# Squared-ReLU layers with seven block products for eight, the weight sums on GpSimd

## The chip, the cores and the metric

The kernel runs on one core of a Trainium2 chip. The metric is the device time of one execution in microseconds (us), the median of several runs. Engines: TensorE (PE; PEld is its weight load), VectorE (DVE), ScalarE (ACT), GpSimd (POOL) and SyncE (SP), which issues the weight loads.

## The reference, cut to what matters

A chain of transformer blocks works on 256 tokens of width 1024. Two of its layers, one behind the latent and neighbourhood attention and one behind the dilated attention, are these:

```python
def sq_relu_mlp(xn, w1, w2):
    return jnp.square(jax.nn.relu(xn @ w1)) @ w2
...
x = x + sq_relu_mlp(rms_norm_2(x, norm_mlp[layer]), mlp_w1[layer], mlp_w2[layer])
```

w1 is 1024 x 4096, w2 is 4096 x 1024, all in float32. After the second layer comes a last norm.

## The kernel before, in words

Every product is kept near float32 accuracy by splitting both operands into a high part (fp32r) and the rest: `split_mm` (L1876 to L1881) issues high x high, high x low and low x high, each a matmul with a weight load of its own. ScalarE makes the high part of a weight tile with a copy (`high`, L627, the copy on L630), VectorE makes the low part by subtracting it from the raw tile (`low`, on L1056).

A squared layer (`mlp(l)`, on each engine) runs in 16 stages of 256 hidden channels. In a stage, `up` makes 256 hidden channels x 256 tokens: 2 halves x 8 blocks of the width x 3 = 48 matmuls of 256 columns, into bank 4 or 5. ScalarE applies the ReLU (L907); VectorE squares it, copies it to fp32r and subtracts (`split_hidden`, L1317, L1318, L1056). `down` multiplies the two 128-token tiles by the two 128-channel blocks and the two 512-column halves of the output, 8 block products x 3 = 24 matmuls of 512 columns. They add up in banks 0 to 3 over the 16 stages. `up` of one stage stands ahead of `down` of the stage before, so that the hidden values are made while TensorE is at work.

The raw weights of a stage are 2 MB in two loads; they lie in one of 4 slots of `weight_pool`. SyncE fetches them (`fetch_ring`) in the order written out; a slot is free once VectorE has made the low part of the down weights (`loD_ready`). High and low parts lie in `work`, two stages deep. In a step ScalarE makes the up weights two stages ahead, then, once `w_used` tells that `down` of the stage before is over, the down weights one stage ahead. VectorE follows it.

After the last stage `update(n, t)` (L1509) adds the banks to the residual, tile by tile, each with the scale of the tokens from the raw norm. The first half of it runs during the last `down` (`y_half`). Then TensorE turns the residual (`turn_raw`), ScalarE and VectorE write it as high and low (`raw_high`, `raw_low`), and the next part starts: dilated attention behind the first layer, the last norm and the output behind the second. On ScalarE and VectorE the first weights of the dilated attention, `od_high(0, 0, 0)` and `od_low(0, 0, 0)`, stand ahead of that update. GpSimd has no work in the two layers.

## Time and profile before

| | us |
|---|---|
| median of 3 runs | 1247.07 |
| lowest, highest | 1246.1, 1250.47 |
| profiled execution, its own time | 1248.23 |
| its span, first to last instruction | 1246.3 |
| TensorE busy in the span | 1184.4 (95%) |
| VectorE busy | 732.6 (59%) |
| ScalarE busy | 547.1 (44%) |
| GpSimd busy | 52.9 (4%) |

The median is the figure to compare. The span leaves out what lies around the first and the last instruction. Matmuls are pipelined, so the duration of one is longer than the time from its start to the next one's; a stage of TensorE is read from starts. An average over the span hides that the parts of the kernel have different limits.

### The profile page before, as it was taken

What the parts mean: (1) busy time and instruction counts of PE and PEld (TensorE: products, weight loads), DVE (VectorE), ACT (ScalarE), POOL (GpSimd) and SP (SyncE); (2) the same over time, 40 slices, a digit from 0 to 9 for tenths busy, and PEclk for the clock granted to TensorE, in tenths of its full rate; (3) what the DMA queues carried; (4) which work ended last, traced back from release to release, by engine and by line L of the source; (5) the groups of instructions that cost most, each with busy time, mean ns of one, the idle gap of its engine ahead of it and who ended that gap; (6) DMA issues with size and microseconds to landing.
All of it is one profiled execution on the core that took longest, in us unless ns stands there. A gap on an engine that the chain in (4) does not pass through costs nothing.

```text
span 1246.3 us, 18678 instructions
## 1 busy us (share of the span) xinstructions
PE 1184.4 (95%) x7356; PEld 1014.8 (81%) x7359; DVE 732.6 (59%) x971; ACT 547.1 (44%) x723; POOL 52.9 (4%) x60
## 2 busy tenths in 40 slices
PE   3899998999999989899999999999999999999997
PEld 1477785689999978647999998999999984999996
DVE  1569336474555576755465466777777765654653
ACT  3763243353434362644343345555555534433432
POOL 2000023000000070000000000000000000000000
PEclk9999999999999989999999999999999999999999
DMA  9673470899565550616645534455555254645410
GB/s 320 237 271 115 166 270 7 288 246 288 173 182 159 160 150 1 233 38 238 209 172 190 186 102 136 124 147 152 151 151 147 77 198 161 244 162 205 175 64 34
DMA packets 201039, 209.71 MB, mean 168 GB/s; under 512 B 5804, under 2 KB 166839, under 8 KB 200791
## 3 DMA queue, kind: packets, MB, share of 16 engines
q1 hardware_dynamic: 197520, 201.61, 51.2%
q0 software_dynamic: 1648, 5.03, 1.4%
q10 hardware_dynamic: 1814, 2.30, 0.6%
q8 instruction: 39, 0.64, 0.3%
q14 instruction: 18, 0.14, 0.0%
HBM read 207.86 MB, written 2.01 MB: 168 GB/s over the span
## 4 chain that ended last, share of the span: by engine, by line
PE 86%; DVE 7%; DMA 4%; ACT 2%; issue 2%; DVEq 0%; SPq 0%; ACTq 0%
PE bank L1879 21%; PE bank L1880 21%; PE bank L1881 21%; DMA weight_pool<-in_mod_w_dram 4%; PE bank L1726 3%; PE bank L1728 3%; PE bank L1727 3%; PE bank L2133 2%; PE bank L2274 2%; PE bank L2262 1%; PE bank L2252 1%; DVE work L1448 1%; PE bank L1683 1%; PE bank L2243 1%; PE bank L2233 1%
## 5 line engine op out<-in xcount | busy, mean ns | idle before, releaser
L1879 PE MATMUL bank<-hT_high,mlp_up_high 128*128 128x256 f32 x512 | 145.2, 284 | 1.1 <-DVE hT_low L1350 1.1
L1881 PE MATMUL bank<-hT_high,mlp_up_low 128*128 128x256 f32 x512 | 144.9, 283 | 0.0
L1880 PE MATMUL bank<-hT_low,mlp_up_high 128*128 128x256 f32 x512 | 144.9, 283 | 0.0
L1879 PE MATMUL bank<-od_w_high,hT_high 128*128 128x384 f32 x384 | 132.7, 346 | 1.6 <-DVE hT_low L1350 1.4
L1881 PE MATMUL bank<-od_w_high,hT_low 128*128 128x384 f32 x384 | 128.7, 335 | 0.0
L1880 PE MATMUL bank<-od_w_low,hT_high 128*128 128x384 f32 x384 | 128.5, 335 | 0.0
L1056 DVE TENSOR_TENSOR mlp_down_low<-weight_pool,mlp_down_high 128x2048 fp32r<-128x2048 f32 x32 | 73.3, 2289 | 59.2 <-ACT mlp_down_high L630 59.2
L1879 PE MATMUL bank<-hT_high,ffn_up_high 128*128 128x256 f32 x352 | 99.7, 283 | 2.0 <-DVE hT_low L1056 2.0
L1879 PEld LDWEIGHTS bank<-hT_high,mlp_up_high 128*128 128x128 f32 x512 | 98.1, 192 | 3.0 <-issue 2.0
L1879 PE MATMUL bank<-mlp_down_high,hidden_high 128*128 128x512 f32 x256 | 99.9, 390 | 0.0
L1880 PE MATMUL bank<-mlp_down_low,hidden_high 128*128 128x512 f32 x256 | 99.9, 390 | 0.0
L1881 PE MATMUL bank<-hT_high,ffn_up_low 128*128 128x256 f32 x352 | 99.6, 283 | 0.0
L1880 PE MATMUL bank<-hT_low,ffn_up_high 128*128 128x256 f32 x352 | 99.6, 283 | 0.0
L1881 PE MATMUL bank<-mlp_down_high,hidden_low 128*128 128x512 f32 x256 | 99.6, 389 | 0.0
L1880 PEld LDWEIGHTS bank<-hT_low,mlp_up_high 128*128 128x128 f32 x512 | 98.2, 192 | 0.8
L1881 PEld LDWEIGHTS bank<-hT_high,mlp_up_low 128*128 128x128 f32 x512 | 98.2, 192 | 0.0
L1056 DVE TENSOR_TENSOR od_w_low<-weight_pool,od_w_high 128x3072 fp32r<-128x3072 f32 x24 | 80.5, 3356 | 28.8 <-ACT od_w_high L630 28.8
L630 ACT ACTIVATE mlp_down_high<-weight_pool 128x2048 fp32r<-128x2048 f32 x32 | 61.2, 1912 | 70.9 <-PE bank L1881 70.9
L907 ACT ACTIVATE work<-bank 128x512 f32<-128x512 f32 x32 | 19.2, 598 | 137.7 <-PE bank L1881 137.7
L1879 PEld LDWEIGHTS bank<-od_w_high,hT_high 128*128 128x128 f32 x384 | 72.1, 188 | 5.5 <-issue 3.2
L1056 DVE TENSOR_TENSOR mlp_up_low<-weight_pool,mlp_up_high 128x2048 fp32r<-128x2048 f32 x32 | 73.2, 2289 | 3.3 <-ACT mlp_up_high L630 3.3
L1317 DVE TENSOR_TENSOR work<-work 128x512 f32<-128x512 f32 x32 | 22.1, 690 | 89.4 <-ACT work L907 89.4
(318 smaller groups left out, 2628.7 us busy)
## 6 DMA issues: line engine op xcount, KB each, us to landing
weight_pool<-in_mlp_w_dram SPq DMA_DIRECT2D x64, 1024.0 KB, 7.4
weight_pool<-in_od_w_in_dram SPq DMA_DIRECT2D x72, 512.0 KB, 5.2
weight_pool<-in_mod_w_dram SPq DMA_DIRECT2D x22, 1024.0 KB, 10.1
weight_pool<-in_ffn_w_in_dram SPq DMA_DIRECT2D x44, 512.0 KB, 6.0
weight_pool<-in_gla_w_in_dram SPq DMA_DIRECT2D x12, 1024.0 KB, 6.4
weight_pool<-in_ffn_w_out_dram SPq DMA_DIRECT2D x22, 512.0 KB, 7.0
weight_pool<-in_gla_w_out_dram SPq DMA_DIRECT2D x2, 2048.0 KB, 15.5
weight_pool<-in_ev_w_in_dram SPq DMA_DIRECT2D x4, 1024.0 KB, 6.6
```

Of the source, the lines that this page charges most:

```text
L630: act.activation(dst[:, :], pool[:, e.at + off:e.at + off + dst.shape[1]], ACT.Copy).then_inc(s[done], 1)
L907: act.activation(act_a[:, j % 2, :], bank[4 + j % 2][:, :], ACT.Relu).then_inc(s["ff_act"], 1)
L1056: dve.tensor_tensor(dst, whole, high.bitcast(F32), ALU.subtract).then_inc(s[done], 1)
L1317: chain(dve.tensor_tensor(whole, *product, ALU.mult))
L1726: mm(out_, left[0], right[0], start=start, stop=False)
L1727: mm(out_, left[0], right[1], start=False, stop=False)
L1728: return mm(out_, left[1], right[0], start=False, stop=stop)
L1879: mm(out_, left[0], right[0], start=start, stop=False, **flag)
L1880: mm(out_, left[0], right[1], start=False, stop=False, **flag)
L1881: return mm(out_, left[1], right[0], start=False, stop=stop, **flag)
L2133: ins = mm(bank[b][:, :], oT[:, k, P * t:P * t + P], pv(e)[:, k % 4, 512 * (b % 2):512 * (b % 2) + 512], start=(k == 4), stop=(k == 3))
L2274: ins = mm(bank[b][:, :], odT[:, k, P * t:P * t + P], pv(e)[:, k % 4, 512 * (b % 2):512 * (b % 2) + 512], start=(k == 0), stop=(k == KD - 1))
```

## The change

`down` uses seven block products for eight (Strassen's scheme in Winograd's form). With the two token tiles and the two channel blocks of the squared hidden values as one 2x2 matrix, and the two channel blocks and two column halves of the down weights as the other, sums of blocks are multiplied. `SEVEN` lists for each product the right operand (`down`: a raw block, `mixed`: one of four sums) and the left one (`squares_high`/`_low`, seven blocks of 128). Each product adds up over the 16 stages in a bank of its own, 0 to 6. `up` has bank 7 alone.

In every stage VectorE makes three more blocks of sums of the squares (L1664, L1666, L1667), and the high and low parts are 896 wide. GpSimd makes the four sums of the weights (three instructions, 1024, 512 and 512 wide; L571, L574, L576) and the low part of the three raw blocks (1536 wide, L579). ScalarE copies 1536 of the raw weights and 2048 of the sums; VectorE subtracts for the sums. Low parts are written over the raw weights in the pool, and a slot is free only after `down` (`w_used`). The products are put together behind the layer (`seven_update`, `seven_out`, and three additions on GpSimd). Dilated attention's weights lie at 6144 on in the pool.

```diff
+        upL = [over(f"mlp_up_slot{j}_low", "weight_pool", 4096 * j, 2048) for j in range(MLP_RING)]
...
+        downL = [over(f"mlp_down_slot{j}_low", "weight_pool", 4096 * j + 2560, 1536) for j in range(MLP_RING)]
+        mixedH = [over(f"mlp_sums{j}_high", "work", at + 1536, 2048) for j, at in enumerate(DOWN_AT)]
+        mixedL = [over(f"mlp_sums{j}_low", "work", at + 3584, 2048) for j, at in enumerate(DOWN_AT)]
+        mixed = [work[:, at + 3584:at + 5632] for at in DOWN_AT]
...
-                L["mlp", l].append(plan(f"mlp{l}_{st}", 4096 * ((st + 2 * l) % MLP_RING),
+                L["mlp", l].append(plan(f"mlp{l}_{st}", 4096 * (st % MLP_RING),
                                         [(0, (KD, 256), w1v[l][:, :, st, :]), (2048, (2, D), w2v[l][:, st, :, :])],
-                                        ("loD_ready", FFC + 16 * l + st + 1),
+                                        ("w_used", FFC + 16 * l + st + 1),
...
-        L["od"] = [plan(f"od{g}", 3072 * g, [(1024 * j, (KD, P), odin[:, :, g, j, m, :]) for j in range(3)],
+        L["od"] = [plan(f"od{g}", 6144 + 3072 * g, [(1024 * j, (KD, P), odin[:, :, g, j, m, :]) for j in range(3)],
...
+        SEVEN = (("down", 0, 0), ("mixed", 2, 5), ("mixed", 1, 3), ("mixed", 3, 1), ("mixed", 0, 4), ("down", 2, 2), ("down", 1, 6))
...
+            def mlp_sums(l, r, j):
+                e, per = L["mlp", l][j % MLP_RING], 16 * 2
+                raw, dst = pool[:, e.at + 2048:e.at + 4096], mixed[j % 2]
+                g.wait_ge(e.sem, r * per + (e.value + per * (j // MLP_RING)))
+                g.tensor_tensor(dst[:, 0:1024].rearrange("p (a c) -> p a c", a=2), raw[:, 0:512].unsqueeze(1).to_broadcast([P, 2, 512]),
+                                raw[:, 512:1536].rearrange("p (a c) -> p a c", a=2), ALU.subtract).then_inc(s["sums_ready"], 1)
+                g.wait_ge(s["sums_ready"], r * 16 + (64 * l + 4 * j + 1))
+                g.tensor_tensor(dst[:, 1024:1536], dst[:, 512:1024], raw[:, 512:1024], ALU.subtract).then_inc(s["sums_ready"], 1)
+                g.wait_ge(s["sums_ready"], r * 16 + (64 * l + 4 * j + 2))
+                g.tensor_tensor(dst[:, 1536:2048], dst[:, 1024:1536], raw[:, 1536:2048], ALU.add).then_inc(s["sums_ready"], 1)
+                g.wait_ge(s["sums_ready"], r * 16 + (64 * l + 4 * j + 3))
+                g.wait_ge(s["hiD_ready"], r * 8 + (FFC + 32 * l + 2 * j + 1))
+                g.tensor_tensor(downL[j % MLP_RING][:, :], raw[:, 512:2048], downH[j % 2][:, :].bitcast(F32), ALU.subtract).then_inc(s["sums_ready"], 1)
+            def mlp(l):
+                mlp_sums(l, 0, 0)
+                with g.Fori(0, MLP_LOOPS - 1) as i:
...
+                n, right = 3 + 2 * l, [res[:, 1, 0:512], res[:, 1, 512:1024]]
+                for i, (h, op) in enumerate(((1, ALU.add), (0, ALU.add), (0, ALU.subtract))):
+                    g.wait_ge(s["seven_out"], 4 * l + i + 2)
+                    if i == 2:
+                        g.wait_ge(s["seven_rest"], 3 * l + 2)
+                    g.tensor_tensor(right[h], right[h], ends[3 + i], op).then_inc(s["seven_rest"], 1)
...
+                act.wait_ge(s["sums_ready"], r * 16 + (64 * l + 4 * j + 3))
+                act.activation(mixedH[j % 2][:, :], mixed[j % 2], ACT.Copy).then_inc(s["hiD_ready"], 1)
...
-                high(mlU[0][0], e[0], 0, e[0].value, "hiU_ready")
-                high(mlD[0][0], e[0], 2048, e[0].value, "hiD_ready")
-                high(mlU[1][0], e[1], 0, e[1].value, "hiU_ready")
+                up_high(l, 0, 0)
+                down_high(l, 0, 0)
+                up_high(l, 0, 1)
+                mixed_high(l, 0, 0)
...
+            def seven_out(l):
+                scale = seven_scale(3 + 2 * l, 1)
+                act.wait_ge(s["seven_ps"], 6 * l + 1)
+                act.activation(ends[0], bank[0][:, :], ACT.Copy).then_inc(s["seven_out"], 1)
+                act.activation(ends[3], bank[0][:, :], ACT.Copy, scale=scale).then_inc(s["seven_out"], 1)
+                act.wait_ge(s["seven_sum"], l + 1)
+                act.activation(ends[4], ends[1], ACT.Copy, scale=scale).then_inc(s["seven_out"], 1)
+                act.wait_ge(s["seven_ps"], 6 * l + 5)
+                act.activation(ends[5], bank[4][:, :], ACT.Copy, scale=scale).then_inc(s["seven_out"], 1)
...
-                    act.wait_ge(s["ff_mid"], st - 1)
-                    act.activation(act_a[:, j % 2, :], bank[4 + j % 2][:, :], ACT.Relu).then_inc(s["ff_act"], 1)
-                    if n_up:
-                        e = first[(j + 2) % MLP_RING]
-                        high(mlU[j % 2][0], e, 0, r * per + (e.value + per * ((j + 2) // MLP_RING)), "hiU_ready")
+                    act.activation(positive, bank[7][:, :], ACT.Relu).then_inc(s["ff_act"], 1)
+                    act.wait_ge(s["squares_whole"], r * MLP_RING + (16 * l + j + 1))
+                    act.wait_ge(s["w_used"], st - 1)
+                    act.activation(sqr2[0][j % 2][:, :], squares[:, P:1024], ACT.Copy).then_inc(s["squares_high"], 1)
                     if n_down:
                         act.wait_ge(s["w_used"], st)
-                        e = first[(j + 1) % MLP_RING]
-                        high(mlD[(j + 1) % 2][0], e, 2048, r * per + (e.value + per * ((j + 1) // MLP_RING)), "hiD_ready")
+                        down_high(l, r, j + 1)
+                    if n_up:
+                        up_high(l, r, j + 2)
+                    if n_down:
+                        mixed_high(l, r, j + 1)
...
-            od_high(0, 0, 0, ("loD_ready", FFC + 16))
+            od_high(0, 0, 0, ("w_used", FFC + 14))
             act.activation(stat[:, 92:93], eps, ACT.Sqrt)
+            seven_out(0)
...
+                if t == 0:
+                    dve.wait_ge(s["seven_out"], 4 * l + 1)
+                    landed_product(2)
+                    dve.tensor_tensor(ends[1], bank[1][:, :], ends[0], ALU.add).then_inc(s["seven_sum"], 1)
+                    dve.wait_ge(s["seven_sum"], l + 1)
+                    landed_product(3)
+                    chain(dve.tensor_tensor(ends[2], bank[2][:, :], ends[1], ALU.subtract))
+                    add(right, ends[2]).then_inc(s["dve_chain"], 1)
+                    add(left, ends[2]).then_inc(s["dve_chain"], 1)
+                    chain.k += 2
+                    landed_product(4)
+                    dve.wait_ge(s["dve_chain"], chain.base + chain.k - 1)
+                    add(right, bank[3][:, :])
+                    dve.wait_ge(s["seven_out"], 4 * l + 4)
+                    dve.wait_ge(s["dve_chain"], chain.base + chain.k)
+                    ins = add(left, bank[4][:, :])
+                else:
+                    landed_product(6)
+                    dve.wait_ge(s["seven_rest"], 3 * l + 3)
+                    add(right, bank[5][:, :])
+                    landed_product(7)
+                    ins = add(left, bank[6][:, :])
...
-                    dve.wait_ge(s["w_used"], st - 1)
-                    split_hidden(j, 512, (act_a[:, j % 2, :], act_a[:, j % 2, :]))
+                    dve.wait_ge(s["ff_mid"], st)
+                    chain(dve.tensor_tensor(squares[:, 0:512], positive, positive, ALU.mult))
+                    chain(dve.tensor_tensor(squares[:, 512:768].rearrange("p (a c) -> p a c", a=2), squares[:, 128:384].rearrange("p (a c) -> p a c", a=2),
+                                            squares[:, 0:128].unsqueeze(1).to_broadcast([P, 2, P]), ALU.add))
+                    chain(dve.tensor_tensor(squares[:, 768:896], squares[:, 640:768], squares[:, 128:256], ALU.add))
+                    dve.tensor_tensor(squares[:, 896:1024], squares[:, 768:896], squares[:, 384:512], ALU.add).then_inc(s["squares_whole"], 1)
+                    dve.wait_ge(s["squares_whole"], r * MLP_RING + (16 * l + j + 1))
+                    dve.wait_ge(s["squares_high"], r * MLP_RING + (16 * l + j + 1))
+                    low(sqr2[1][j % 2][:, :], squares[:, P:1024], sqr2[0][j % 2][:, :], "ff_mid")
                     if n_up:
-                        low_weights(mlU[j % 2], first[(j + 2) % MLP_RING], 0, "hiU_ready", st + 3, "loU_ready")
+                        up_low(l, r, j + 2)
                     if n_down:
-                        low_weights(mlD[(j + 1) % 2], first[(j + 1) % MLP_RING], 2048, "hiD_ready", st + 2, "loD_ready")
+                        mixed_low(l, r, j + 1)
...
-                    for t in range(NT):
-                        for f, b in ((0, 2 * t), (0, 2 * t + 1), (1, 2 * t), (1, 2 * t + 1)):
-                            at = D * f + 512 * (b % 2)
-                            ins = split_mm(bank[b][:, :], both(mid2, lambda x: x[:, j % 2, 256 * f + P * (b // 2):256 * f + P * (b // 2) + P]),
-                                           both(mlD[j % 2], lambda x: x[:, at:at + 512]), False, last and f == 1, running=True)
-                        if last and t == 0:
-                            ins.then_inc(s["y_half"], 1)
+                def down(r, j, last=False):
+                    pe.wait_ge(s["ff_mid"], r * MLP_RING + (FFC + 16 * l + j + 1))
+                    pe.wait_ge(s["loD_ready"], r * MLP_RING + (FFC + 16 * l + j + 1))
+                    pe.wait_ge(s["sums_ready"], r * 16 + (64 * l + 4 * j + 4))
+                    halves = {"down": (downH[j % 2], downL[j % MLP_RING]), "mixed": (mixedH[j % 2], mixedL[j % 2])}
+                    for b, (which, i, left) in enumerate(SEVEN):
+                        ins = split_mm(bank[b][:, :], both((sqr2[0][j % 2], sqr2[1][j % 2]), lambda x: x[:, P * left:P * left + P]),
+                                       both(halves[which], lambda x: x[:, 512 * i:512 * i + 512]), False, last, running=True)
+                        if last and b < 6:
+                            ins.then_inc(s["seven_ps"], 1)
                     ins.then_inc(s["w_used"], 1)
...
+                with pe.Fori(0, MLP_LOOPS - 1) as i:
                     for j in range(MLP_RING):
-                        up(st + j, j)
-                        if j:
```

**VectorE, one stage** (the unrolled stages of the first layer). `work<-work` of 512 is the square; `hidden_low` and `squares_low` are the low parts of the squares, `mlp_up_low` and `mlp_up_slot_low` of the up weights, `mlp_sums_low` of the weight sums. Before:

```order
L1317 TENSOR_TENSOR work<-work 128x512 [waits w_used,ff_act]
L1318 CAST hidden_high<-work 128x512 [waits dve_chain]
L1056 TENSOR_TENSOR hidden_low<-work,hidden_high 128x512 [waits dve_chain]
L1056 TENSOR_TENSOR mlp_up_low<-weight_pool,mlp_up_high 128x2048 [waits hiU_ready]
L1056 TENSOR_TENSOR mlp_down_low<-weight_pool,mlp_down_high 128x2048 [waits hiD_ready]
```

and now:

```order
L1663 TENSOR_TENSOR work<-work 128x512 [waits ff_mid,ff_act]
L1664 TENSOR_TENSOR work<-work 128x256 [waits dve_chain]
L1666 TENSOR_TENSOR work<-work 128x128 [waits dve_chain]
L1667 TENSOR_TENSOR work<-work 128x128 [waits dve_chain]
L1140 TENSOR_TENSOR squares_low<-work,squares_high 128x896 [waits squares_high,squares_whole]
L1140 TENSOR_TENSOR mlp_up_slot_low<-weight_pool,mlp_up_high 128x2048 [waits hiU_ready]
L1140 TENSOR_TENSOR mlp_sums_low<-work,mlp_sums_high 128x2048 [waits hiD_ready]
```

The cast has gone to ScalarE, three additions have come in, and every one of the seven instructions reads two operands from SBUF.

**GpSimd, the last stage of the first layer and what follows it.** Before, these are its last instructions, none of them in a squared layer:

```order
L545 DMA work<-bias_copies 64x8x64 [waits w_used]
L545 DMA work<-bias_copies 64x8x64 x15
L550 TENSOR_TENSOR work<-work,consts 128x512 [waits consts_loaded,bias_loaded]
L550 TENSOR_TENSOR work<-work,consts 128x512 x7
L552 DMA consts<-in_norm_final_dram 128x1024 [waits o_out]
```

and now, with the weight sums, the low part of the raw blocks and the additions to the residual:

```order
L571 TENSOR_TENSOR work<-weight_pool 128x1024 [waits w_mlp3,w_used]
L574 TENSOR_TENSOR work<-work,weight_pool 128x512 [waits sums_ready]
L576 TENSOR_TENSOR work<-work,weight_pool 128x512 [waits sums_ready]
L579 TENSOR_TENSOR mlp_down_slot_low<-weight_pool,mlp_down_high 128x1536 [waits hiD_ready,sums_ready]
L596 TENSOR_TENSOR residual<-residual,work 128x512 [waits seven_out] x2
L596 TENSOR_TENSOR residual<-residual,work 128x512 [waits seven_rest,seven_out]
L601 DMA consts<-in_norm_final_dram 128x1024 [waits o_out]
```

Four such instructions stand in each of the 32 stages, where none was.

**VectorE, the end of the first layer** (`od_w_low` is the dilated attention's first weights). Before:

```order
L1056 TENSOR_TENSOR hidden_low<-work,hidden_high 128x512 [waits dve_chain]
L1056 TENSOR_TENSOR od_w_low<-weight_pool,od_w_high 128x3072 [waits od_hi]
L1509 SCALAR_TENSOR_TENSOR residual<-bank,stat,residual 128x512 [waits y_half]
L1509 SCALAR_TENSOR_TENSOR residual<-bank,stat,residual 128x512
L1509 SCALAR_TENSOR_TENSOR residual<-bank,stat,residual 128x512 [waits w_used,res_ready]
L1509 SCALAR_TENSOR_TENSOR residual<-bank,stat,residual 128x512
```

and now:

```order
L1140 TENSOR_TENSOR squares_low<-work,squares_high 128x896 [waits squares_high,squares_whole]
L1140 TENSOR_TENSOR od_w_low<-weight_pool,od_w_high 128x3072 [waits od_hi]
L1611 TENSOR_TENSOR work<-bank,work 128x512 [waits seven_ps,seven_out]
L1614 TENSOR_TENSOR work<-bank,work 128x512 [waits seven_ps,seven_sum]
L1602 SCALAR_TENSOR_TENSOR residual<-work,stat,residual 128x512 [waits dve_chain]
L1602 SCALAR_TENSOR_TENSOR residual<-work,stat,residual 128x512
L1602 SCALAR_TENSOR_TENSOR residual<-bank,stat,residual 128x512 [waits dve_chain,seven_ps]
L1602 SCALAR_TENSOR_TENSOR residual<-bank,stat,residual 128x512 [waits dve_chain,seven_out]
L1602 SCALAR_TENSOR_TENSOR residual<-bank,stat,residual 128x512 [waits seven_rest,seven_ps,res_ready]
L1602 SCALAR_TENSOR_TENSOR residual<-bank,stat,residual 128x512 [waits w_used]
L1434 SCALAR_TENSOR_TENSOR hT_low<-bank,vecB,hT_high 128x256 [waits hT_hi,res_ready]
```

`od_w_low` stands ahead of eight instructions of the update where it stood ahead of four. On SyncE its three loads now wait for `w_used` of stage 14 (`down` of the last stage but one), since their place overlaps slots 1 and 2; before, they waited for `loD_ready`.

## Rows read from the trace of the kernel before

**Rows 1.** Part 1 of the page: busy time, share, instructions of the engines.
```profile
PE 1184.4 (95%) x7356; PEld 1014.8 (81%) x7359; DVE 732.6 (59%) x971; ACT 547.1 (44%) x723; POOL 52.9 (4%) x60
```

**Rows 2.** Windows over the two squared layers: us, then busy time of each engine, clock, DMA.
```profile
573.60:753.60 180.00, 179.93 (x1155) 164.62 (x1156) 100.88 (x88) 70.61 (x56) 0.00 (x0) 1.00 0.57 190
1059.20:1239.60 180.40, 179.81 (x1152) 164.22 (x1152) 97.95 (x88) 68.27 (x56) 0.00 (x0) 1.00 0.42 147
```

**Rows 3.** Waits inside the first layer: total us, times, longest us.
```profile
ACT work L907 <- PE bank L1881: 68.8, 16, 9.4
DVE work L1317 <- ACT work L907: 44.7, 12, 7.8
```

**Rows 4.** Timeline, TensorE, one stage: start us, duration us, instruction.
```profile
630.26 0.40 PE L1879 MATMUL bank<-mlp_down_high,hidden_high 128*128 128x512 f32 x1
...
635.73 0.28 PE L1879 MATMUL bank<-hT_high,mlp_up_high 128*128 128x256 f32 x1
...
641.48 0.40 PE L1879 MATMUL bank<-mlp_down_high,hidden_high 128*128 128x512 f32 x1
```

**Rows 5.** Groups by shape, VectorE: busy us, mean ns of one, idle before.
```profile
L1056 DVE TENSOR_TENSOR mlp_down_low<-weight_pool,mlp_down_high 128x2048 fp32r<-128x2048 f32 x32 | 73.3, 2289 | 59.2 <-ACT mlp_down_high L630 59.2
...
L1056 DVE TENSOR_TENSOR ffn_down_low<-weight_pool,ffn_down_high 128x1024 fp32r<-128x1024 f32 x22 | 26.8, 1219 | 2.2 <-ACT ffn_down_high L630 2.2
...
L1056 DVE TENSOR_TENSOR hidden_low<-work,hidden_high 128x512 fp32r<-128x512 f32 x32 | 22.2, 692 | 1.1
...
L1389 DVE TENSOR_TENSOR work<-work 128x256 f32<-128x256 f32 x48 | 20.4, 425 | 1.6
...
L1389 DVE TENSOR_TENSOR work<-work 128x128 f32<-128x128 f32 x4 | 1.2, 292 | 0.1
```

**Rows 6.** Groups by shape, ScalarE.
```profile
L630 ACT ACTIVATE mlp_down_high<-weight_pool 128x2048 fp32r<-128x2048 f32 x32 | 61.2, 1912 | 70.9 <-PE bank L1881 70.9
...
L630 ACT ACTIVATE ffn_down_high<-weight_pool 128x1024 fp32r<-128x1024 f32 x22 | 23.3, 1058 | 11.2 <-PE bank L1881 11.2
```

**Rows 7.** GpSimd's two long shapes, by tile and line: min/median/max ns.
```profile
L532 POOL TENSOR_TENSOR gla_out_low<-weight_pool,gla_out_high x6: 2362/2377/2387, 184.0 to 202.4; 128x1024 fp32r<-128x1024 f32 x6
...
L550 POOL TENSOR_TENSOR work<-work,consts x8: 1275/1287/3268, 455.1 to 465.8; 128x512 f32<-128x512 f32 x8
```

**Rows 8.** Timeline, GpSimd, while the mask is added (window from 454 us).
```profile
455.11 3.27 POOL L550 TENSOR_TENSOR work<-work,consts 128x512 f32<-128x512 f32 x1 [3.08 <-DMA work<-bias_copies]
...
463.34 2.54 POOL L550 TENSOR_TENSOR work<-work,consts 128x512 f32<-128x512 f32 x2
```

**Rows 9.** Timeline, VectorE, in the same stretch.
```profile
452.74 4.49 DVE L1056 TENSOR_TENSOR ev_w_low<-weight_pool,ev_w_high 128x2048 fp32r<-128x2048 f32 x2 [1.64 <-ACT ev_w_high L630]
...
463.35 1.33 DVE L1385 TENSOR_TENSOR work<-work,consts 128x32 f32<-128x32 f32 x1
...
464.71 1.21 DVE L1389 TENSOR_TENSOR work<-work 128x32 f32<-128x32 f32 x1
...
467.10 0.18 DVE L1385 TENSOR_TENSOR work<-work,consts 128x32 f32<-128x32 f32 x1
```

**Rows 10.** Windows around a pause of TensorE: PE busy first, PEclk after POOL.
```profile
440.00:450.00 10.00, 5.50 (x25) 4.33 (x24) 7.84 (x15) 7.62 (x23) 8.90 (x14) 0.78 0.66 165
520.00:535.00 15.00, 11.55 (x86) 6.82 (x82) 14.48 (x40) 10.66 (x35) 0.00 (x0) 1.00 0.89 321
```

**Rows 11.** Timeline at the end of the first layer, three engines.
```profile
743.12 2.77 ACT L630 ACTIVATE od_w_high<-weight_pool 128x3072 fp32r<-128x3072 f32 x1
...
745.92 3.36 DVE L1056 TENSOR_TENSOR od_w_low<-weight_pool,od_w_high 128x3072 fp32r<-128x3072 f32 x1 [0.79 <-ACT od_w_high L630]
...
753.61 1.41 DVE L1509 SCALAR_TENSOR_TENSOR residual<-bank,stat,residual 128x512 f32<-128x512 f32 x2 [1.38 <-PE bank L1881]
...
757.57 0.41 PE L1879 MATMUL bank<-od_w_high,hT_high 128*128 128x384 f32 x1 [1.41 <-DVE hT_low L1350]
```

**Rows 12.** DMA issues, dilated attention's weights: KB each, us to landing.
```profile
weight_pool<-in_od_w_in_dram SPq DMA_DIRECT2D x72, 512.0 KB, 5.2
```

148 lines of the change are left out of this document (90 added, 58 removed).

## The prediction, as put on record before the changed kernel ran

> **What bounds the kernel now.** I read the page's part 1 first: TensorE is busy 95% of the span, GpSimd 4% [rows 1]. That is an average, so next come the windows over the two squared layers: 180.0 and 180.4 us, TensorE busy in all but 0.1 and 0.6 us, at a granted clock of 1.00 (2.4 GHz), VectorE for 100.9 and 98.0, GpSimd for nothing [rows 2]. The waits say the same from the other side: ScalarE waited 16 times, 68.8 us, for TensorE's last `up` matmul, and VectorE for ScalarE behind it [rows 3]. So TensorE's issue is the limit, and an instruction there costs its distance from start to start. The timeline gives it: 24 `down` matmuls from 630.26 to 635.73 are 5.47 us, 0.228 each; 48 `up` matmuls to 641.48 are 5.75 us, 0.120 each [rows 4]. A stage is 11.22 us, 16 are 179.5.
>
> **What goes from TensorE.** Per stage 3 of 24 `down` matmuls: 3 x 0.228 = 0.68 us. A stage of TensorE alone would be 10.54 us; over 32 stages 21.9 us go, if nothing else takes longer than 10.54. Three more zeroing matmuls a layer are under 1 us each and are left at nothing. The rest of the prediction is on that "if".
>
> **VectorE per stage.** Durations are from [rows 5]: square of 512, 0.69; sums of 256, 128 and 128, 0.43 + 0.29 + 0.29; the low part of 896, between 0.69 (512) and 1.22 (1024), 1.09; the low parts of the up weights and of the sums, 2.29 each. Sum 7.37 us, where it was 100.9 / 16 = 6.3 [rows 2]. ScalarE, by [rows 6], 1.91 + 1.91 for the two of 2048, 1.49 for 1536, 0.94 for 896 (both interpolated), and the ReLU as before: under 7 us. Neither is a bound by itself.
>
> **GpSimd per stage.** 1024 elements took 2.38 us and 512 took 1.29 [rows 7], so 2.13 us per 1000 elements more, and 1536 take 3.47. The four instructions are 2.38 + 1.29 + 1.29 + 3.47 = 8.43 us. Alone that fits into 10.54 too.
>
> **The two together don't.** The rows that decide are of another stage, the only one where GpSimd computes while VectorE has instructions with two operands in SBUF. GpSimd's addition of 512 that began at 455.11 took 3.27 us instead of 1.29 [rows 7, 8]. VectorE's `ev_w_low`, two SBUF operands, ran until 452.74 + 4.49 = 457.23 [rows 9]: GpSimd got nothing until then. The other way round, VectorE's additions over 32 elements took 1.33 and 1.21 us, where the same one took 0.18 at 467.10; GpSimd's additions ran from 463.34 to 465.88, and each small one ended with one of them [rows 8, 9]. So an instruction of either waits for the whole of the other's. All seven of VectorE's in a stage have two operands in SBUF (the cast, which had one, is gone), and all four of GpSimd's. They go one after another: 7.37 + 8.43 = 15.80 us per stage, and this is the new bound.
>
> **The order adds pauses.** A stage on this shared path, as the waits of the program order it: low part of the sums 2.29, GpSimd 1.29, square 0.69, GpSimd 1.29, three sums 1.01; then nothing can use it while ScalarE copies the squares (0.94); low part of the squares 1.09; a pause of 0.40, since GpSimd's last instruction waits for ScalarE's copy of 1536, which took 1.49 from the same moment; GpSimd 3.47, low part of the up weights 2.29, GpSimd's first of the next stage 2.38. Sum 17.14. Against that, the instruction that had waited at 455.11 ended at 458.38, 0.13 less than 1.29 behind 457.23: the start of an instruction is hidden in the wait. With up to seven that wait, 0.9 us come off: 16.2. I take 16.6, between the two, since the rows show one such start only.
>
> A page of the Trainium skill speaks against the 0.13: "SBUF — State Buffer", section "SBUF: two separate sides", says that VectorE (with two SBUF inputs) and GpSimd share a port pair under an exclusive lock held for the whole instruction. That the other one blocks, the trace agrees with (3.27 and 1.33 us above). By the page every duration would count whole, 17.1 per stage, and both layers would come out 15 us longer than I take.
>
> **Sum for a layer.** First stage: `up` 5.75, then about 11 until the end of the first `down` (`up` 5.75, `down` 21 x 0.228 = 4.8, a little wait). Then 14 stages of 16.6 = 232.4. The last: no weights to prepare, so ReLU, squares, copy and low part, some 5.3 us, then `down` 4.8: 10.1. Together 259.3 against 180.1: +79.2 us a layer, +158.4 for both. TensorE, with 10.5 us of work in 16.6, no longer matters.
>
> **The seams.** (1) Behind the first layer, `od_w_high` and `od_w_low` stand ahead of the update. They ran at 743.12 and 745.92, ten us before the last `down` ended [rows 11], so the load was long in. Now the three loads wait for `down` of stage 14. One landed 5.2 us after issue [rows 12], three in one queue I put at 6.5; then 2.77 + 3.36 us: 12.6 us behind that `down`, where the last `down` ends at 10.1. Then eight instructions of the update instead of a last one of two: at 1.41 for two [rows 11] 5.6 us, and up to one of GpSimd's additions, 1.29, between them. The residual is complete some 9.4 us behind the last `down`; before, at 755.02, some 1.6 behind it. What follows to 757.57 stays. +7.8 us. (2) Ahead of the second layer GpSimd's first sums and VectorE's first low parts meet on the shared path; nothing in [rows 1 to 12] shows it, the bounds are 0 (covered by the attention's out product) and one chain of 2.38 + 1.29 + 1.29 + 3.47 = 8.4. I take 2, nearer to the cover, which is some 16 us long. (3) At the very end eight instructions stand for four, but most run during the last `down`: between 0 and 5.6, I take 2.5. Seams together +12.3.
>
> **Sum.** +158.4 + 12.3 = +170.7 us. The profiled execution took 1248.23 (its span 1246.3), 1.2 above the median of 1247.07. 1248.2 + 170.7 = 1418.9 for a profiled execution, **1418 us** for the median.
>
> **Bounds.** Lower: the shared path packed without a pause and with 0.13 off at each of 11: 15.80 - 1.43 = 14.4 per stage, 228 a layer, seams 8: 1247 + 96 + 8 = 1351. Upper: 17.14 and one us of stumbling per stage, 18.1, 280 a layer, seams 20: 1247 + 200 + 20 = 1467.
>
> **Rival 1, faster: the shared path does not bind.** This is so if these shapes do not shut each other out, so that the path's load is under 10.54 us per stage. Against it stand the five durations in [rows 8, 9]; for it, that they are few and that the small ones read another tile. Then TensorE keeps the bound: 1247.1 - 21.9 + 12.3 = 1237 us. A neighbour of it ends at no change: there is a ring through both engines, squares 1.69, copy 0.94, copy of 1536 1.49, of 2048 1.91, low part 2.29, low part of the sums 2.29 and back to the squares, 10.6 us and some 0.2 for the hand-overs. At 10.8 a stage the layers give 3.6 us each and the seams take 9: 1249 us.
>
> **Rival 2, slower still: TensorE's clock.** In the window 440 to 450, with TensorE busy 5.5 of 10 us, the granted clock was 0.78, so partly the lower of its two levels, 1.2 GHz; with 11.55 of 15 us busy it stayed at 1.00 [rows 10]. In the new stages TensorE has work for 10.5 of 16.6 us, between the two. If it stayed at 1.2 GHz all through, a stage would be 2 x 10.54 = 21.1 us, a layer 337, and the kernel 1247 + 2 x 157 + 12 = 1573. If only part of a stage is at the lower level, the slower matmuls fill pauses of 6 us, and it costs little; that case is in my range.
>
> The Trainium skill, "TensorE: Matmul & The Clock Gate", section "What's actually happening", holds that idleness throttles the array to half its clock and activity releases it. By this rule a stage with a long pause starts slow; a slower TensorE is a busier one, though, which is why I don't put the kernel there.
>
> **Chances.** Shared path as the bound, 1418: 0.87. TensorE bound, 1237: 0.05. Ring, 1249: 0.04. Clock, up to 1573: 0.04. Half a per cent, 6.2 us, is about what a measurement of this kernel can tell from no change. Faster 0.05, same 0.04, slower 0.91. The range is 1360 to 1470: it leaves out the three other cases (0.13) and a little of the lower bound.
>
> **What would show it.** In the new profile: GpSimd and VectorE busy for nearly all of a squared layer, with their durations stretched (means above 2.29 for the 2048 low parts, far above 1.29 for the 512 sums); TensorE idle for 6 us in each stage, waiting for VectorE's low parts; stages near 16.6 us; ScalarE's copies unchanged. If GpSimd's four show 2.38, 1.29, 1.29 and 3.47 at their medians and TensorE has no pause, the main step is wrong. If stages are 14 or 18, the pauses or hand-overs are mis-sized. At the first seam `od_w_high` should wait for its load.

## The result and the profile after

The changed kernel took **1410.25 us** (median of 4 runs, 1406.57 to 1411.84) beside 1247.76 for the kernel before on the same chip: ratio 1.1296, 95% interval 1.1264 to 1.1327. The forecast was 1418 us, range 1360 to 1470, slower with a chance of 0.91. The profiled execution has a span of 1407.5 us, 161.2 more than the 1246.3 of before.

Part 1 of the page, the line that answers to [rows 1]:

```profile
PE 1224.2 (87%) x7269; PEld 1036.5 (74%) x7269; DVE 940.5 (67%) x1043; ACT 620.2 (44%) x795; POOL 379.9 (27%) x194
```

GpSimd now works 379.9 us in place of 52.9, and VectorE is "busy" 940.5 in place of 732.6 with about one more microsecond of work per stage. Busy time here contains waiting.

Windows over the two squared layers, to be read beside [rows 2] (us, then busy time of PE, PEld, DVE, ACT, POOL, then granted clock, DMA share, GB/s):

```profile
573.20:825.00 251.80, 199.23 (x1107) 174.73 (x1107) 193.00 (x117) 98.11 (x83) 139.67 (x57) 0.88 0.36 122
1146.20:1397.90 251.70, 200.27 (x1107) 175.69 (x1107) 195.93 (x121) 102.10 (x88) 141.77 (x59) 0.87 0.30 103
```

Each layer is 252 us where it was 180. TensorE, which had no gap before, is busy 199 of 252, at a granted clock of 0.88 and 0.87 where it was 1.00.

The waits inside the first layer, where [rows 3] had TensorE as the one that is waited for (total us, times, longest us):

```profile
ACT squares_high L989 <- DVE work L1667: 143.6, 16, 9.8
...
PE bank L2012 <- DVE squares_low L1140: 52.5, 15, 4.0
POOL work L571 <- PE bank L2014: 47.0, 14, 4.3
```

TensorE waits for VectorE's low part of the squares, 15 times in 16 stages. What VectorE does in a stage is in its timeline (start us, duration us, instruction, and in brackets the idle time before it):

```profile
650.80 3.88 DVE L1140 TENSOR_TENSOR mlp_up_slot_low<-weight_pool,mlp_up_high 128x2048 fp32r<-128x2048 f32 x1 [2.02 <-ACT mlp_up_high L681]
654.60 2.28 DVE L1140 TENSOR_TENSOR mlp_sums_low<-work,mlp_sums_high 128x2048 fp32r<-128x2048 f32 x1
656.81 2.88 DVE L1663 TENSOR_TENSOR work<-work 128x512 f32<-128x512 f32 x1
659.72 1.40 DVE L1664 TENSOR_TENSOR work<-work 128x256 f32<-128x256 f32 x1
661.16 1.27 DVE L1666 TENSOR_TENSOR work<-work 128x128 f32<-128x128 f32 x1
662.46 0.29 DVE L1667 TENSOR_TENSOR work<-work 128x128 f32<-128x128 f32 x1
663.84 1.09 DVE L1140 TENSOR_TENSOR squares_low<-work,squares_high 128x896 fp32r<-128x896 f32 x1 [1.08 <-ACT squares_high L989]
666.94 3.88 DVE L1140 TENSOR_TENSOR mlp_up_slot_low<-weight_pool,mlp_up_high 128x2048 fp32r<-128x2048 f32 x1 [2.01 <-ACT mlp_up_high L681]
```

And GpSimd in the same stage:

```profile
649.04 3.49 POOL L579 TENSOR_TENSOR mlp_down_slot_low<-weight_pool,mlp_down_high 128x1536 fp32r<-128x1536 f32 x1 [2.99 <-ACT mlp_down_high L681]
656.73 2.42 POOL L571 TENSOR_TENSOR work<-weight_pool 128x1024 f32<-128x1024 f32 x1 [4.20 <-PE bank L2014]
659.22 1.62 POOL L574 TENSOR_TENSOR work<-work,weight_pool 128x512 f32<-128x512 f32 x1
660.92 1.35 POOL L576 TENSOR_TENSOR work<-work,weight_pool 128x512 f32<-128x512 f32 x1
665.18 3.48 POOL L579 TENSOR_TENSOR mlp_down_slot_low<-weight_pool,mlp_down_high 128x1536 fp32r<-128x1536 f32 x1 [2.91 <-ACT mlp_down_high L681]
```

Four of VectorE's seven instructions are stretched: 3.88 for 2.29, 2.88 for 0.69, 1.40 for 0.43, 1.27 for 0.29. The other three (2.28, 0.29 and 1.09) have the length that they have alone. Read the ends together: GpSimd's 1536 ends at 652.53, and `mlp_up_slot_low` at 654.68, 2.15 later. GpSimd's 1024 ends at 659.15, the square at 659.69, GpSimd's next at 660.84, the sum of 256 at 661.12, GpSimd's last sum at 662.27, the sum of 128 at 662.43. Each step but the first is one instruction that waited for the one before it, and it is shorter than that instruction alone by 0.11 to 0.15 us (between 654.68 and 659.15 VectorE's unhindered low part of the sums ends too, at 656.88). One stage is 16.14 us, from 650.80 to 666.94. In the order of this path, from the end of one low part of the squares to the next: 0.25 pause, 3.49, 2.15, 2.20, 2.27, 0.54, 1.15, 0.28, 1.15, 0.16, 0.32, 1.09 pause for ScalarE's copy, 1.09. That is 16.14, with 1.34 of it pause.

TensorE in the same stage: the first `down` matmul, the 13th, the first one of `up`, and the next `down`:

```profile
648.92 0.79 PE L2012 MATMUL bank<-mlp_down_high,squares_high 128*128 128x512 f32 x1 [3.81 <-DVE squares_low L1140]
...
654.20 0.55 PE L2012 MATMUL bank<-mlp_sums_high,squares_high 128*128 128x512 f32 x1
...
656.40 0.28 PE L2012 MATMUL bank<-hT_high,mlp_up_high 128*128 128x256 f32 x1
...
665.06 0.79 PE L2012 MATMUL bank<-mlp_down_high,squares_high 128*128 128x512 f32 x1 [2.74 <-DVE squares_low L1140]
```

`down` takes 7.48 us here where 21 matmuls at the pace of [rows 4] would be 4.8: the first 13 start 0.43 us apart (0.59 behind the very first), the last 8 are 0.227 apart. The granted clock is 0.50 between 648.9 and 654.0 and 1.00 between 654.6 and 656.4, so the array is at 1.2 GHz for the first part, after 3.8 us without work, and at 2.4 GHz from then on. `up` runs at 0.120 as before. The slow part isn't the same in every stage. In the 14 stages between the first and the last it is 6 to 14 matmuls of a `down`, behind pauses of 2.5 to 4.0 us, and the last `down` has none, behind 3.2. The stages are 16.1 to 16.2 us long all the same, which already speaks against the clock as their limit.

The seam behind the first layer, ScalarE's and VectorE's rows that answer to [rows 11]:

```profile
824.88 2.76 ACT L681 ACTIVATE od_w_high<-weight_pool 128x3072 fp32r<-128x3072 f32 x1 [6.00 <-DMA weight_pool<-in_od_w_in_dram]
```

```profile
827.67 3.36 DVE L1140 TENSOR_TENSOR od_w_low<-weight_pool,od_w_high 128x3072 fp32r<-128x3072 f32 x1 [7.60 <-ACT od_w_high L681]
...
832.39 2.42 DVE L1602 SCALAR_TENSOR_TENSOR residual<-work,stat,residual 128x512 f32<-128x512 f32 x2
834.74 2.84 DVE L1602 SCALAR_TENSOR_TENSOR residual<-bank,stat,residual 128x512 f32<-128x512 f32 x4
```

The last `down` ended at 825.18, the residual was complete at 837.58, and the attention's first matmul came at 840.64.

### The profile page after: what moved, and what is told of

It is laid out like the page before. It is cut to its first block, busy times and chain, and to the rows that moved or that the text cites. A ratio compares the mean times of both kernels' runs of the same rounds, so it can differ in the third digit from the quotient of the medians.

```text
span 1407.5 us, 19139 instructions
## 1 busy us (share of the span) xinstructions
PE 1224.2 (87%) x7269; PEld 1036.5 (74%) x7269; DVE 940.5 (67%) x1043; ACT 620.2 (44%) x795; POOL 379.9 (27%) x194
## 4 chain that ended last, share of the span: by engine, by line
PE 48%; DVE 26%; issue 11%; ACT 9%; DMA 4%; POOL 1%; ACTq 0%; DVEq 0%; SPq 0%; POOLq 0%
PE bank L2012 11%; PE bank L2014 10%; PE bank L2013 10%; DVE work L1663 5%; DVE mlp_sums_low L1140 5%; ACT mlp_up_high L681 4%; DMA weight_pool<-in_mod_w_dram 3%; DVE work L1664 3%; ACT mlp_down_high L681 3%; DVE work L1666 3%; PE bank L2266 2%; PE bank L1859 1%; PE bank L1861 1%; PE bank L1860 1%; PE bank L2397 1%
## 5 line engine op out<-in xcount | busy, mean ns | idle before, releaser
L1140 DVE TENSOR_TENSOR mlp_up_slot_low<-weight_pool,mlp_up_high 128x2048 fp32r<-128x2048 f32 x32 | 121.9, 3811 | 60.3 <-ACT mlp_up_high L681 60.3
L989 ACT ACTIVATE squares_high<-work 128x896 fp32r<-128x896 f32 x32 | 30.4, 949 | 287.3 <-DVE work L1667 287.3
L571 POOL TENSOR_TENSOR work<-weight_pool 128x1024 f32<-128x1024 f32 x32 | 105.5, 3298 | 177.7 <-PE bank L2014 94.4
L2014 PE MATMUL bank<-hT_high,mlp_up_slot_low 128*128 128x256 f32 x512 | 144.8, 283 | 0.0
L579 POOL TENSOR_TENSOR mlp_down_slot_low<-weight_pool,mlp_down_high 128x1536 fp32r<-128x1536 f32 x32 | 111.8, 3493 | 108.9 <-ACT mlp_down_high L681 108.7
L2012 PE MATMUL bank<-mlp_down_high,squares_high 128*128 128x512 f32 x96 | 45.5, 474 | 103.8 <-DVE squares_low L1140 103.8
L2012 PEld LDWEIGHTS bank<-mlp_down_high,squares_high 128*128 128x128 f32 x96 | 19.6, 204 | 112.9 <-issue 81.8
L2014 PEld LDWEIGHTS bank<-hT_high,mlp_up_slot_low 128*128 128x128 f32 x512 | 98.1, 192 | 0.0
L1140 DVE TENSOR_TENSOR mlp_sums_low<-work,mlp_sums_high 128x2048 fp32r<-128x2048 f32 x32 | 79.0, 2470 | 10.2 <-ACT mlp_sums_high L954 10.2
L1663 DVE TENSOR_TENSOR work<-work 128x512 f32<-128x512 f32 x32 | 79.1, 2472 | 8.7 <-ACT work L986 8.7
## 6 DMA issues: line engine op xcount, KB each, us to landing
weight_pool<-in_gla_w_out_dram SPq DMA_DIRECT2D x2, 2048.0 KB, 15.5
```

The costliest lines, as they stand in the source:

```text
L571: g.tensor_tensor(dst[:, 0:1024].rearrange("p (a c) -> p a c", a=2), raw[:, 0:512].unsqueeze(1).to_broadcast([P, 2, 512]), raw[:, 512:1536 ...
L579: g.tensor_tensor(downL[j % MLP_RING][:, :], raw[:, 512:2048], downH[j % 2][:, :].bitcast(F32), ALU.subtract).then_inc(s["sums_ready"], 1)
L989: act.activation(sqr2[0][j % 2][:, :], squares[:, P:1024], ACT.Copy).then_inc(s["squares_high"], 1)
L1140: dve.tensor_tensor(dst, whole, high.bitcast(F32), ALU.subtract).then_inc(s[done], 1)
L1663: chain(dve.tensor_tensor(squares[:, 0:512], positive, positive, ALU.mult))
L2012: mm(out_, left[0], right[0], start=start, stop=False, **flag)
```

## Where the 161 us are

Cut at TensorE's first `up`, its last `down`, and the attention's first matmul: the first layer went from 573.67 to 753.49 and goes from 573.24 to 825.18; the second from 1059.29 to 1239.10 and now from 1146.27 to 1398.22. That is +72.1 each, +144.3. The seam behind the first layer was 4.1 and is 15.5, +11.4. From there to the second layer 301.7 became 305.6, +3.9. The end was 7.2 and is 9.3, +2.1; the start is 0.4 earlier. Sum +161.3, 0.1 off by rounding. (The first `up` starts between 571.8 and 577.1 in the traces of the other runs, so one or two us between single traces say little.)

## The experiments

Three theories were held against each other. **Shared path:** an instruction of VectorE with two operands in SBUF and one of GpSimd shut each other out for their whole length, and the sum of both engines' work, plus pauses, is the stage. **Clock:** the stage is long because each `down` starts at TensorE's lower level, as the rows above now show. **Late chain:** GpSimd and VectorE don't block each other, and the four instructions with their hand-overs are simply late.

### 1. GpSimd's work left out

```diff
-                mlp_sums(l, 0, 0)
...
-                act.wait_ge(s["sums_ready"], r * 16 + (64 * l + 4 * j + 3))
-                act.activation(mixedH[j % 2][:, :], mixed[j % 2], ACT.Copy).then_inc(s["hiD_ready"], 1)
+                e, landed_at = mlp_high(l, r, j)
+                high(mixedH[j % 2], e, 2048, landed_at, "hiD_ready")
...
-                low(mixedL[j % 2][:, :], mixed[j % 2], mixedH[j % 2][:, :], "loD_ready")
+                low(mixedL[j % 2][:, :], pool[:, e.at + 2048:e.at + 4096], mixedH[j % 2][:, :], "loD_ready")
...
-                    halves = {"down": (downH[j % 2], downL[j % MLP_RING]), "mixed": (mixedH[j % 2], mixedL[j % 2])}
+                    halves = {"down": (downH[j % 2], upL[j % MLP_RING]), "mixed": (mixedH[j % 2], mixedL[j % 2])}
```

> GpSimd's four instructions of each stage are left out: the low part of the down weights is not made (the up weights' low part stands in its place) and the mixed weights are copies of the raw ones, so that VectorE, ScalarE and TensorE have the same instructions as in the changed kernel, and the sums are not computed. Shared path theory (GpSimd and VectorE's two-operand instructions shut each other out): the path loses 8.43 us a stage, what is left is the ring of ScalarE and VectorE at about 10.8 us, so 28 stages shorten from 16.13 to 10.8, 149 us, and the start of the second layer gives back 4: 1257 us (1240 to 1275), and VectorE's durations go back to 2.29, 0.69, 0.43 and 0.29. Clock theory (the stage is long because each down starts at TensorE's lower clock): the slow matmuls stay, a stage stays above 13 us, above 1320 us.

Measured: 1246.6 us (8 runs), ratio to before 0.9976, interval 0.9959 to 0.9993. VectorE's timeline:

```profile
648.50 2.29 DVE L1132 TENSOR_TENSOR mlp_up_slot_low<-weight_pool,mlp_up_high 128x2048 fp32r<-128x2048 f32 x1 [2.01 <-ACT mlp_up_high L673]
...
652.91 0.68 DVE L1656 TENSOR_TENSOR work<-work 128x512 f32<-128x512 f32 x1
...
658.91 2.29 DVE L1132 TENSOR_TENSOR mlp_up_slot_low<-weight_pool,mlp_up_high 128x2048 fp32r<-128x2048 f32 x1 [2.02 <-ACT mlp_up_high L673]
```

The durations are back to 2.29 and 0.68, a stage is 10.41 us here, and the clock theory's 1320 is out: `down` is as slow only as long as there are pauses ahead of it (mean granted clock of the run 0.986, where the changed kernel had 0.943). The late chain isn't ruled out by this run, since its instructions are gone too. The run says a second thing. Here the seven products have all they need for nothing, and the kernel is 0.2% faster than before, not 22 us: a layer is 170.2 us in place of 179.8, and 14.4 us are lost in the seam behind the first. Within the layers TensorE is the limit again: it is busy for all of the 160 us between 580 and 740, at a granted clock of 1.00, and VectorE for 108.5. The 10.41 us are the time of its own 69 matmuls.

### 2. TensorE kept busy

```diff
-                def up(r, j):
+                def up(r, j, halves=(0, 0, 1)):
...
-                    for f in range(2):
+                    for f in halves:
...
-                up(0, 0)
+                up(0, 0, (0, 1))
```

> The first half of each up product but a layer's first is computed twice, 24 more matmuls or 2.9 us of TensorE in its pause of about 3 us, same result. Clock theory: TensorE has no pause, the down matmuls run at 0.228 instead of 0.427 for 13 of 21, 2.6 us a stage come back, 28 stages, 73 us: 1337 us. Shared path theory: the granted clock rises to 1.00 and down gets shorter, but GpSimd's first sum then only waits for VectorE's low part of the sums in place of TensorE; the stage stays at 16.1: 1410 us (1402 to 1418).

Measured: 1411.06 us (1408.45 to 1413.8), ratio 1.1299. Windows over 160 us of the first layer, first this kernel, then the changed one:

```profile
620.00:780.00 160.00, 137.89 (x922) 124.20 (x921) 129.45 (x68) 61.42 (x48) 111.83 (x40) 1.00 0.38 131
```

```profile
620.00:780.00 160.00, 126.35 (x688) 110.81 (x687) 127.83 (x71) 62.66 (x51) 94.04 (x41) 0.85 0.38 131
```

The granted clock is 1.00 in place of 0.85, and nothing is gained. TensorE still pauses, by 1.5 us ahead of `down` and 0.8 ahead of `up`. The stages are 16.3 us. Where the time that `down` gave back went is in VectorE's row and GpSimd's: GpSimd's first sum stands earlier in line and lengthens another instruction.

```profile
657.94 4.49 DVE L1140 TENSOR_TENSOR mlp_sums_low<-work,mlp_sums_high 128x2048 fp32r<-128x2048 f32 x1
```

```profile
657.46 2.82 POOL L571 TENSOR_TENSOR work<-weight_pool 128x1024 f32<-128x1024 f32 x1 [1.58 <-PE bank L2014]
```

The slow clock in the changed kernel goes with the pauses: shorter pauses, no slow matmuls. It costs nothing there, since the path of VectorE and GpSimd is longer either way.

### 3. One instruction moved to VectorE

```diff
-                g.tensor_tensor(downL[j % MLP_RING][:, :], raw[:, 512:2048], downH[j % 2][:, :].bitcast(F32), ALU.subtract).then_inc(s["sums_ready"], 1)
...
+                low(downL[j % MLP_RING][:, :], pool[:, e.at + 2560:e.at + 4096], downH[j % 2][:, :], "silc_zeroed")
```

> The low part of the down weights (1536 wide) moves from GpSimd (3.47 us) to VectorE (about 1.75). Shared path theory: only the sum of both engines counts, so a stage falls by 3.47 - 1.75 = 1.72 and perhaps the 0.40 pause ahead of it: 28 stages, 48 to 59 us: 1358 us (1345 to 1368). Rival, the two engines do not block each other and GpSimd's chain of four is simply late: GpSimd has 4.96 us a stage left, VectorE 9.1, and the stage falls to the ring, about 10.8 to 11.5: 1257 to 1277 us.

Measured: 1360.97 us (2 runs), ratio 1.0905. By the spans (1407.5 and 1359.2) that is 1.73 us for each of 28 stages, where 3.47 - 1.75 is 1.72; so close a match is luck. From stage to stage most are 14.5 us, some stand in threes of 12.6, 15.4 and 13.6, and the mean is 14.2: 1.9 us less than 16.14, between the 1.72 and the 2.12 with the 0.40 pause. The two layers got 54 us shorter, and the start, the seams and the end gave 6 back. VectorE got more work and the kernel 48 us faster. The late chain's 1257 to 1277 is out: with 4.96 us of GpSimd in a stage the stage is still 14.2.

### 4. All of it on VectorE

```diff
+                    if n_up:
+                        up_low(l, r, j + 2)
                     dve.wait_ge(s["squares_whole"], r * MLP_RING + (16 * l + j + 1))
...
                     if n_down:
+                        dve.wait_ge(s["w_used"], st)
+                        mlp_sums(l, r, j + 1)
+                        down_low(l, r, j + 1)
                         mixed_low(l, r, j + 1)
```

The order changes too: as in number 7 below, the up weights' low part now stands ahead of that of the squares, and their high part ahead of ScalarE's copy.

> All four of GpSimd's instructions move to VectorE (1.22 + 0.69 + 0.69 + 1.75 = 4.35 us), in an order in which VectorE always has something ready. Shared path theory: nothing is shared any more, VectorE alone bounds the stage with 7.37 + 4.35 = 11.72 us and some 0.3 between dependent instructions, 12.0: 28 stages x 4.13 = 116 us and 4 at the second layer's start: 1290 us (1275 to 1310), still slower than before the change (a stage of 11.22). Rival, a stage is bound by the order of hand-overs and not by a sum of durations: no gain or a small one, above 1350 us.

Measured: 1286.01 us (1284.86 to 1290.01), ratio 1.0313. VectorE's first sum, from stage to stage:

```profile
655.52 1.22 DVE L1628 TENSOR_TENSOR work<-weight_pool 128x1024 f32<-128x1024 f32 x1
...
658.22 1.76 DVE L1117 TENSOR_TENSOR mlp_down_slot_low<-weight_pool,mlp_down_high 128x1536 fp32r<-128x1536 f32 x1
660.18 2.29 DVE L1117 TENSOR_TENSOR mlp_sums_low<-work,mlp_sums_high 128x2048 fp32r<-128x2048 f32 x1 [0.20 <-ACT mlp_sums_high L931]
...
667.30 1.22 DVE L1628 TENSOR_TENSOR work<-weight_pool 128x1024 f32<-128x1024 f32 x1
```

11.78 us, of which 0.20 is the only idle time: VectorE is the bound. The same instructions that take 16.14 us on two engines take 11.78 on one. Not all of the 4.36 is the move. By number 7 the order alone brings 1.2. The work that is moved is 4.35 us there in place of 8.43, 4.08 less, and against it stand seven hidden starts of 0.13, which only blocked instructions have: 3.2 us by this estimate, and 16.14 - 1.2 - 3.2 = 11.7 is close to the 11.78 measured.

### 5. GpSimd beside the kernel before, with two operands, one, or none

The changed kernel's two engines share data and semaphores. In these three nothing is shared: GpSimd works on a scratch tile of its own, nobody waits for it, and the kernel is the one before.

```diff
+            def beside(l):
+                for i in range(14):
+                    g.wait_ge(s["w_used"], i + (FFC + 16 * l + 1))
+                    for m, n in enumerate((512,) * 7):
...
+                        g.tensor_tensor(scratch[:, 0:n], scratch[:, 0:n], scratch[:, 0:n], ALU.mult).then_inc(s["zero_ready"], 1)
```

The other two have `g.memset(scratch[:, 0:n], 0.0)` and `g.tensor_scalar(scratch[:, 0:n], scratch[:, 0:n], 1.0, None, ALU.mult)` in the last line.

> The kernel before, with seven products of a scratch tile of 512 with itself on GpSimd beside each of 14 stages of each squared layer; nothing waits for them, same result. Shared path theory: GpSimd always has one pending, so each two-operand instruction of VectorE waits for up to 1.15 us of it: low parts of 2048 rise from 2.29 to about 3.4, square and low part of the hidden layer from 0.69 to about 1.8, GpSimd's from 1.29 to between 1.9 and 3.4; VectorE's cast (one operand) stays at 0.43. VectorE goes from 6.4 to some 11 us a stage, next to TensorE's 11.22: the time rises by 0 to 15 us. Rival, the stretched durations of the changed kernel come from its semaphores or tiles (both engines there work on the same tile): here nothing is shared, all durations stay, same time.

> As the one with two operands, but GpSimd fills the scratch tile with a constant (no operand in SBUF is read). If only a GpSimd instruction that reads SBUF shuts VectorE's two-operand instructions out, VectorE stays at 2.29 and 0.69 and GpSimd's fill keeps one duration; if any GpSimd instruction does, VectorE's are stretched by up to one fill each.

> As the run with two operands on GpSimd, but its seven instructions a stage have one operand (the scratch tile times a constant). If reading SBUF is what counts, VectorE's durations rise as there (2048 to about 3.1, 512 to 1.2 to 1.5, the cast of 512 to 1.15); if two operands are needed on both sides, they stay at 2.29, 0.69 and 0.43.

Groups by shape between 600 and 740 us (count, busy us, mean ns of one), first with two operands on GpSimd:

```profile
L560 POOL TENSOR_TENSOR scratch<-scratch 128x512 f32<-128x512 f32 x78 | 135.1, 1732 | 7.3 <-PE bank L1894 0.7
...
L1069 DVE TENSOR_TENSOR mlp_up_low<-weight_pool,mlp_up_high 128x2048 fp32r<-128x2048 f32 x12 | 37.5, 3123 | 0.0
...
L1069 DVE TENSOR_TENSOR mlp_down_low<-weight_pool,mlp_down_high 128x2048 fp32r<-128x2048 f32 x12 | 36.6, 3046 | 0.8 <-ACT mlp_down_high L643 0.8
...
L1069 DVE TENSOR_TENSOR hidden_low<-work,hidden_high 128x512 fp32r<-128x512 f32 x12 | 16.9, 1411 | 0.4
L1330 DVE TENSOR_TENSOR work<-work 128x512 f32<-128x512 f32 x12 | 14.7, 1224 | 23.6 <-ACT work L920 23.6
L1331 DVE CAST hidden_high<-work 128x512 fp32r<-128x512 f32 x12 | 13.8, 1149 | 0.4
```

with the fill:

```profile
L560 POOL MEMSET scratch<- 128x512 f32 x88 | 46.3, 526 | 97.7 <-PE bank L1894 93.4
...
L1069 DVE TENSOR_TENSOR mlp_up_low<-weight_pool,mlp_up_high 128x2048 fp32r<-128x2048 f32 x12 | 27.5, 2289 | 0.0
...
L1331 DVE CAST hidden_high<-work 128x512 fp32r<-128x512 f32 x12 | 5.1, 428 | 0.4
```

with one operand:

```profile
L560 POOL TENSOR_SCALAR scratch<-scratch 128x512 f32<-128x512 f32 x64 | 136.5, 2133 | 5.9 <-POOL scratch L560 1.4
...
L1069 DVE TENSOR_TENSOR mlp_down_low<-weight_pool,mlp_down_high 128x2048 fp32r<-128x2048 f32 x13 | 31.0, 2386 | 20.9 <-ACT mlp_down_high L643 20.9
L1069 DVE TENSOR_TENSOR mlp_up_low<-weight_pool,mlp_up_high 128x2048 fp32r<-128x2048 f32 x12 | 27.4, 2280 | 0.0
...
L1069 DVE TENSOR_TENSOR hidden_low<-work,hidden_high 128x512 fp32r<-128x512 f32 x12 | 10.9, 906 | 0.4
...
L1331 DVE CAST hidden_high<-work 128x512 fp32r<-128x512 f32 x12 | 6.5, 538 | 0.4
```

Two operands: VectorE's 2.29 became 3.12 and 3.05, its 0.69 became 1.41 and 1.22, with no data in common. That is the mutual exclusion by itself. It isn't a common pace that both engines slow down to: the 2048s rose by 0.8 us and the 512s by 0.5 to 0.7, though the one is more than three times the other, as a wait for one GpSimd instruction makes it. The fill keeps 0.53 us and leaves VectorE at 2.29, also where the two overlap (638.88 to 641.17, with fills from 636.95 to 640.39). The cast went from 0.43 to 1.15, where I had expected it unchanged for its one operand.

One operand was not what either side of the expectation said: GpSimd's mean went to 2.13 us (alone, 1.49), so it waits for VectorE, and VectorE's 2048 of the up weights stayed at 2.28, while that of the down weights rose to 2.39 and the short ones by 0.10 to 0.22. VectorE is blocked by it much less than by the form with two operands. Why the two forms differ stays open.

The times: 1257.56 us with two operands (ratio 1.0059, interval 1.0044 to 1.0073), 1249.19 with the fill (one run). TensorE, the bound of the kernel before, hid most of VectorE's waiting. The 1279.33 us with one operand (one run) aren't a slower kernel: GpSimd's scratch work had fallen behind and ran on to 1274 us, when the rest had been done for 30 us.

### 6. The seam

```diff
+            seven_out(0)
             od_high(0, 0, 0, ("w_used", FFC + 14))
             act.activation(stat[:, 92:93], eps, ACT.Sqrt)
-            seven_out(0)
...
-            od_low(0, 0, 0)
             for t in range(NT):
                 seven_update(0, t)
+            od_low(0, 0, 0)
```

> The changed kernel with the preparation of the dilated attention's first weights moved behind the seven products' update, on ScalarE and VectorE. Seam theory: in the changed kernel the update waits for a load that lands 7.9 us behind the down of the stage before the last; freed of it the residual is complete 3.5 us behind the last down, as at the end of the kernel, in place of 12.4; the weights' low part then ends at about 832 instead of 831, and the attention's first matmul starts some 7 us earlier: 1403 us (1399 to 1406). Rival, the load bounds the seam in either order: no gain, 1410 us.

Measured: 1403.06 us (1401.72 to 1404.78), ratio 1.1228 beside the changed kernel's 1.1296. VectorE finishes the update, and only then takes the weights:

```profile
827.82 2.84 DVE L1602 SCALAR_TENSOR_TENSOR residual<-bank,stat,residual 128x512 f32<-128x512 f32 x4
830.69 3.36 DVE L1140 TENSOR_TENSOR od_w_low<-weight_pool,od_w_high 128x3072 fp32r<-128x3072 f32 x1
```

The wait for the load was on the path of the update and is off it: the seam is 6.9 us in place of 15.5, and the kernel as a whole gains some 7.

### 7. The order within a stage

```diff
                     act.activation(positive, bank[7][:, :], ACT.Relu).then_inc(s["ff_act"], 1)
+                    if n_up:
+                        up_high(l, r, j + 2)
                     act.wait_ge(s["squares_whole"], r * MLP_RING + (16 * l + j + 1))
...
+                    if n_up:
+                        up_low(l, r, j + 2)
                     dve.wait_ge(s["squares_whole"], r * MLP_RING + (16 * l + j + 1))
```

> The changed kernel with the same instructions in another order: ScalarE makes the high part of the next up weights ahead of its copy of the squares, VectorE their low part while that copy runs. Shared path theory: the pauses on the path (0.94 for the copy, 0.40, and the wait for the high parts) are filled, the stage falls from 16.13 to the packed 15.80 less 0.13 for each of ten or eleven hidden starts, 14.4 to 14.6: 28 x 1.6 = 45 us, 1365 us (1355 to 1380). Rival, the ring through TensorE (down, then GpSimd's sums, then the squares' low part, then down) sets the stage: it stays above 15.5, 1393 us or more.

Measured: 1372.9 us (1372.48 to 1373.41), ratio 1.0993. ScalarE's copies of the squares began at 639.89, 650.22 and 669.79: two stages are 29.9 us, 14.95 each, and unequal, since in every second one the low part of the sums waits for its sums:

```profile
652.31 3.30 DVE L1140 TENSOR_TENSOR squares_low<-work,squares_high 128x896 fp32r<-128x896 f32 x1
660.11 3.84 DVE L1140 TENSOR_TENSOR mlp_sums_low<-work,mlp_sums_high 128x2048 fp32r<-128x2048 f32 x1 [4.50 <-ACT mlp_sums_high L954]
```

So 1.2 us a stage come back by order alone, where 1.34 were pause (over all stages of a layer the mean distance is 14.5 us, where the changed kernel has 15.7): within the range of the shared path, and half a microsecond short of the packed 14.4. The TensorE ring's 1393 is out.

### 8. The best of it, and the ceiling

The first kernel is number 4 with the squares made on ScalarE and the seam of number 6; the second is number 1 with that seam.

```diff
-                    chain(dve.tensor_tensor(squares[:, 0:512], positive, positive, ALU.mult))
...
+                    act.activation(squares[:, 0:512], positive, ACT.Square).then_inc(s["pool_zeroed"], 1)
```

> All sums and low parts on VectorE, the squares themselves on ScalarE (0.57 us there, 0.69 off VectorE), and the seam's order of the run before; nothing on GpSimd in the stages. VectorE theory: it bounds the stage at 11.79 now and at 11.1 here, ScalarE has 7.5: 28 stages x 0.69 = 19 us and 7 us of the seam off 1286: 1260 us (1253 to 1268), still no gain over the kernel before, since VectorE's 11.1 is hardly under the 11.22 of a stage before and the seams cost some 10 us. Rival, the ring of hand-overs between ScalarE and VectorE is the bound there: 1275 to 1282 us.

> The run without GpSimd's four instructions (same work left out) with the seam's order of the later run. It has 1246.6 us with a layer of 170.2 in place of 179.9 us, 19.5 for both, and loses 14.5 of them between the last down of the first layer and the attention's first matmul. In the new order that matmul can start 9 us earlier, when the weights' low part and the residual are there: 1238 us (1234 to 1242). It bounds what the seven products could bring if the sums cost nothing: about 10 us. Rival, the load of the attention's weights bounds the seam: 1243 to 1247 us.

Measured: 1262.12 us (6 runs), ratio 1.0111, interval 1.0093 to 1.013. VectorE's first sum began at 628.61 and 639.66, 11.05 apart; a stage before was 11.22. A layer is 184.1 us all the same where it was 179.8, since the stages at its two ends are longer, and another 4 us are lost outside the layers. The ceiling, with no sums at all, is 1239.33 us, ratio 0.9924, interval 0.9907 to 0.9941. There the attention's first matmul came 4.4 us earlier than in number 1 and not 9. The first layer had begun 2.1 us later in this trace, so counted from the last `down` it is 6.5; the rest is the load, which landed at 750.01, 5 us behind that `down`:

```profile
750.01 2.77 ACT L673 ACTIVATE od_w_high<-weight_pool 128x3072 fp32r<-128x3072 f32 x1 [5.34 <-DMA weight_pool<-in_od_w_in_dram]
```

No version that computed the sums beat the kernel before. With this order and layout the sums for nothing bring 0.8% (interval 0.6 to 0.9%), so a version that has to make them would need other changes to gain more; none was tried.

## Why the prediction was right, and where it was off

**The main step held.** "An instruction of either waits for the whole of the other's" was read from five durations of another stage [rows 8, 9]. The changed kernel shows it in every stage, number 5 shows it without any shared data, and the stages of number 3 and 4 follow it to within 0.3 us. GpSimd's four, unhindered, are 3.48, 2.38, 1.27 and 1.26 us against my 3.47, 2.38, 1.29 and 1.29; VectorE's seven in number 1 sum to 7.34 against 7.37.

**The stage: 16.6 forecast, 16.14 measured.** I had 17.14 with pauses and up to 0.9 off for hidden starts, and took the middle. The hidden start of 0.13 was real each time (0.11 to 0.15), so 16.2 was right. The term mis-sized is this choice: 0.46 x 28 = 13 us, most of the miss in the layers (forecast +158.4, measured +144.3). The two pauses I named, 0.94 and 0.40, are 1.09 and 0.25 in the timeline.

**The page on SBUF.** The Trainium skill, "SBUF — State Buffer", section "SBUF: two separate sides", holds the lock for the whole instruction; I had put its reading at 17.1 a stage. The exclusion is as it says, but the measured 16.14 needs 0.11 to 0.15 us of each blocked instruction outside the lock. The same section counts VectorE's two-operand instructions only against a GpSimd instruction that reads SBUF: number 5 agrees in two of three forms (2.29 beside the fill, 3.12 beside two operands). The form with one operand reads SBUF as well, and VectorE's 2048s were only 2.28 and 2.39 beside it; there page and measurement differ, and the measurement decides. The section also names casts among the instructions that can take both of VectorE's ports. The cast of 0.43 that became 1.15 fits that, though no run here shows the mode itself; my expectation had counted operands and left that out.

**TensorE's clock.** Rival 2 was a clock at 1.2 GHz all through, 1573 us. The clock fell to 1.2 GHz, but only for the first 6 to 14 matmuls of a `down`, and number 2 shows that this cost nothing. "TensorE idle for 6 us in each stage" was wrong by it: the pause is 2.5 to 4.0 us, the slower `down` fills the rest.

**Rival 1 and its neighbour.** With the path taken away (number 1) the kernel was at 1246.6, next to the 1249 of the ring and not at 1237. That nearness is luck. A ring at 10.8 us a stage would have shown; the stage is 10.41, and TensorE, never idle there, sets it, as rival 1 has it. The layers gave back 9.6 us each, where I had 3.6 for the ring (a number that 10.8 in place of 11.22 doesn't give either: 14 x 0.42 is 5.9), and everything outside them took 17.5 where I had 9. The distance to 1237 is in the seams.

**The seams: +12.3 forecast, +17.0 measured**, with the 0.4 at the start. Behind the first layer I had +7.8 and it was +11.4. The load took 7.9 us from the end of that `down` (816.94) and not 6.5, the last `down` ended 8.2 behind it and not 10.1, and the update took 6.6 in place of 5.6 plus a part. Ahead of the second layer I had 2 of up to 8.4; it was 3.9. Of this 2.3 go away with the sums (303.4 us there in number 1, 305.6 here), and GpSimd's rows show them at work: with VectorE's low parts beside them its 512s take 3.2 us each. Where the other 1.6 come from stays open.

```profile
1129.06 3.20 POOL L574 TENSOR_TENSOR work<-work,weight_pool 128x512 f32<-128x512 f32 x1
1132.34 3.19 POOL L576 TENSOR_TENSOR work<-work,weight_pool 128x512 f32<-128x512 f32 x1
```

At the very end 2.1 against 2.5. So two errors of opposite sign, 14 us too much in the layers and 5 too little at the seams, leave the total 9.5 us high.

## What to carry to other kernels

Before work with two SBUF operands goes to an idle GpSimd, add its time to that of VectorE's instructions with two SBUF operands in the same stretch; if the sum is above the present bound, it will be the new one, and an idle share of 96% says nothing against that. The same work on VectorE can be cheaper although VectorE is the fuller engine: here 4.35 us a stage replaced 8.43. And price the ceiling first: three of 24 matmuls in a stage looked like 22 us. With all sums free the layers gave 19, and the kernel gained 9, since the new places in the pool let the attention's first load start only behind a `down` near the end, and so put it on the path.

## What the runs showed that I had not expected

- VectorE's cast of 512 from SBUF to SBUF took 1.15 us in place of 0.43 beside GpSimd's products: an instruction with one operand can be shut out as well.
- GpSimd's form with one operand gave way to VectorE: its own mean rose from 1.49 to 2.13 us, VectorE's 2048s were 2.28 and 2.39. The form with two operands made VectorE's wait (3.12) and rose less (1.73, alone 1.29 for an addition of this size).
- In 14 stages of a layer TensorE came back to its higher level within each `down`, after 6 to 14 matmuls 0.43 us apart, though it had been idle for 2.5 to 4.0 us before every one of them; behind 3.2 us of idleness the last `down` ran at the higher level from its start.
